# Product-key queries of three weight blocks as three products of rounded parts, keys behind the next block's half

## The reference, cut to what matters

```python
q = (xf @ wq).reshape(T, PEER_HEADS, 2, PEER_KEY_DIM)
s = jnp.einsum('thcd,ckd->thck', q, subkeys)
sv, si = lax.top_k(s, PEER_TOPK)
cand = (sv[:, :, 0, :, None] + sv[:, :, 1, None, :]).reshape(T, PEER_HEADS, 256)
cv, ci = lax.top_k(cand, PEER_TOPK)
...
act = jax.nn.gelu(jnp.einsum('cd,ced->ce', xc, u_tab[ec]))
return jnp.einsum('ce,ced->cd', act * gc, v_tab[ec])
```

## Time and profile before

| | us |
|---|---|
| median of three runs | 3874.69 (3873.38 to 3875.21) |
| span of the profiled execution | 3869.6 |
| TensorE busy (share of the span) | 3708.4 (96%) |
| VectorE busy | 1932.2 (50%) |
| ScalarE busy | 1122.8 (29%) |
| GpSimd busy | 311.1 (8%) |
| keys and queries of layer 0 | about 196 to 256 |
| same stage of layer 1 | about 1275 to 1334 |

### The profile page before, as it was taken

How to read it: one execution, slowest core, us unless ns; L and a number is a source line. 1 busy time by engine, 2 the same in 40 slices (tenths; PEclk the granted TensorE clock), 3 DMA queues, 4 the chain that set the end, 5 groups by cost and what they waited for, 6 DMA issues and landing times.

```text
span 3869.6 us, 59400 instructions
## 1 busy us (share of the span) xinstructions
PE 3708.4 (96%) x25424; PEld 2645.2 (68%) x25424; DVE 1932.2 (50%) x3543; ACT 1122.8 (29%) x1721; POOL 311.1 (8%) x205
## 2 busy tenths in 40 slices
PE   8999999999999999999999999999899999999997
PEld 7789988898887799889888875666743333332333
DVE  5485667768655865676777424455612111111111
ACT  3223244444433232444444412333210000000011
POOL 0013200000000132000000000112100000000000
PEclk9899999999999999999999999999999999999999
DMA  5535344445545354344455331112379999999996
GB/s 197 216 136 169 131 148 160 175 160 179 174 175 186 142 167 139 135 172 168 160 184 178 135 116 74 68 66 87 113 317 427 427 427 428 428 427 427 428 428 277
DMA packets 81039, 846.48 MB, mean 219 GB/s; under 512 B 8896, under 2 KB 11072, under 8 KB 12512
## 3 DMA queue, kind: packets, MB, share of 16 engines
q1 hardware_dynamic: 80768, 842.60, 55.8%
HBM read 841.52 MB, written 1.05 MB: 218 GB/s over the span
## 4 chain that ended last, share of the span: by engine, by line
PE 80%; DMA 10%; DVE 7%; ACT 2%; issue 1%; POOL 0%; DVEq 0%; ACTq 0%; SPq 0%
PE bank L86 78%; DMA ring<-in_w_gu_dram 10%; DVE arena L122 2%; ACT arena L112 1%; PE bank L99 1%; DVE arena L190 1%; DVE arena L136 1%; DVE arena L184 1%; DVE arena L166 0%; DVE arena L154 0%; DVE arena L196 0%; DVE ring_rounded L122 0%; DVE arena L128 0%; DVE arena L130 0%; DMA ring<-in_w_inA_dram 0%
## 5 line engine op out<-in xcount | busy, mean ns | idle before, releaser
L86 PE MATMUL bank<-arena 128*128 128x32 bf16 (+9 forms) x10068 | 970.5, 297 | 44.1 <-DVE arena L122 17.2
L86 PEld LDWEIGHTS bank<-arena 128*128 128x128 bf16 (+4 forms) x10068 | 550.7, 124 | 458.7 <-issue 335.1
L122 DVE TENSOR_TENSOR arena<-arena 128x512 bf16<-128x512 bf16 (+5 forms) x898 | 559.2, 657 | 53.2 <-ACT arena L112 37.6
L112 ACT ACTIVATE arena<-bank 128x256 f32<-128x256 f32 (+2 forms) x443 | 202.7, 457 | 1272.9 <-PE bank L86 1043.5
L86 PE MATMUL bank<-ring,arena 128*64 128x512 f32 (+1 forms) x1968 | 503.7, 596 | 39.9 <-DMA ring<-in_w_gu_dram 36.2
L86 PE MATMUL bank<-xT,ring 128*128 128x256 f32 (+1 forms) x2208 | 458.1, 365 | 14.3 <-DMA ring<-in_w_inA_dram 11.3
L86 PE MATMUL bank<-xhi,uhi 128*128 128x256 f32 x1552 | 454.3, 293 | 14.5 <-DVE arena L128 8.7
L86 PE MATMUL bank<-xlo,uhi 128*128 128x256 f32 x1552 | 438.2, 282 | 0.0
L86 PE MATMUL bank<-xhi,ring_rounded 128*128 128x256 f32 x1552 | 436.0, 281 | 0.0
L86 PEld LDWEIGHTS bank<-xT,ring 128*128 128x128 f32 x2208 | 388.7, 193 | 60.9 <-issue 11.6
L86 PEld LDWEIGHTS bank<-ring,arena 128*64 128x64 f32 (+1 forms) x1968 | 170.6, 145 | 362.0 <-issue 282.6
(11 more groups left out here) (137 smaller groups left out, 2949.3 us busy)
## 6 DMA issues: line engine op xcount, KB each, us to landing
ring<-in_w_gu_dram SPq DMA_DIRECT2D x97, 2048.0 KB, 23.8
ring<-in_peer_u_dram SPq DMA_DIRECT2D x128, 1024.0 KB, 6.7
ring<-in_peer_v_dram SPq DMA_DIRECT2D x128, 1024.0 KB, 5.1
arena<-in_w_dn_dram SPq DMA_DIRECT2D x62, 2048.0 KB, 22.3
arena<-in_w_gu_dram SPq DMA_DIRECT2D x43, 2048.0 KB, 22.4
ring<-in_w_hg_dram SPq DMA_DIRECT2D x14, 2048.0 KB, 8.2
ring<-in_w_mod_dram SPq DMA_DIRECT2D x12, 2048.0 KB, 8.2
ring<-in_w_inA_dram SPq DMA_DIRECT2D x8, 2048.0 KB, 8.0
```

The lines of the kernel that those rows point to most:

```text
L86: i = self.e.matmul(o, l, r, start=start, stop=stop)
L112: self.e.activation(o, i, f, scale=scale, **kw).then_inc(self.sem, 1)
L122: self.e.tensor_tensor(o, a, b, op).then_inc(self.sem, 1)
```

## The change

The weight blocks 1 to 3 of the queries are multiplied as parts, as the parted expert blocks are: ScalarE copies each half, rounded, to a new place in the arena (`q_hi`, laid over the expert layer's activations, which aren't in use yet), and a subtraction writes the rest over the weights in the ring. VectorE does it for block 1, ahead of its choosing; GpSimd for blocks 2 and 3. TensorE does the keys of a block behind the first half of the next block, and the keys of block 3 behind expert block 0. ScalarE's queue is reordered to fit, and expert blocks 0 and 2 are rounded before block 3's second half of queries.

```diff
+        def pe_query_parts(l, j, hf):
+            b, (s, n) = route_banks.take("q", l, j, hf)
+            P.wait_ge(s, n)
+            P.wait_ge(*at["x split", l])
+            P.wait_ge(*at["wq split", l, j, hf])
+            hi, lo = q_hi[j - 1][:, :, hf * 256:hf * 256 + 256], query_low(l, j, hf)
+            for k in range(2):
+                cs = slice(k * 128, k * 128 + 128)
+                P.mm(b[:, k * 256:k * 256 + 256], [(w[:, dc, cs], x[:, dc, :]) for dc in range(8)
+                                                   for w, x in ((hi, xhi), (hi, xlo), (lo, xhi))])
...
         def pe_peer(l):
             after_stage(P, "mix", l)
-            for j in range(4):
-                for hf in range(2):
-                    pe_query(l, j, None if j else 1, hf)
-                for tk in range(2):
...
+            for hf in range(2):
+                pe_query(l, 0, 1, hf)
+            for j in range(1, 4):
+                pe_query_parts(l, j, 0)
+                pe_keys(l, j - 1)
+                pe_query_parts(l, j, 1)
+            pe_stage1(l, 0)
+            pe_keys(l, 3)
             P.mark("routed", l)
-            P.wait_ge(*at["x split", l])
-            for c in range(TURNED):
+            for c in range(1, TURNED):
                 pe_stage1(l, c)
...
+        def split_query(q, l, j, hf):
+            q.wait_ge(*at["wq high", l, j, hf])
+            q.tt(query_low(l, j, hf), query_of(l, j, hf), q_hi[j - 1][:, :, hf * 256:hf * 256 + 256].bitcast(F32), SUB,
+                 lag=FREE)
+            q.mark("wq split", l, j, hf)
...
             V.mark("x split", l)
+            for hf in range(2):
+                split_query(V, l, 1, hf)
             for j in range(4):
                 dve_choose(l, j)
...
+        def act_split_query(l, j, hf):
+            A.wait_ge(*at["landed", ("wq", l, j)])
+            A.act(q_hi[j - 1][:, :, hf * 256:hf * 256 + 256], query_of(l, j, hf), ACT.Copy)
+            A.mark("wq high", l, j, hf)
...
             A.mark("x high", l)
-            for j in range(4):
...
-            act_split_u(l, 0)
-            act_split_u(l, 2)
+            act_split_query(l, 1, 0)
+            act_query(l, 0, 0)
+            act_split_query(l, 1, 1)
+            act_query(l, 0, 1)
+            for hf in range(2):
+                act_split_query(l, 2, hf)
+            for j in range(1, 4):
+                act_query(l, j, 0)
+                act_key_scores(l, j - 1)
+                if j == 1:
+                    for hf in range(2):
+                        act_split_query(l, 3, hf)
+                if j == 3:
+                    act_split_u(l, 0)
+                    act_split_u(l, 2)
+                act_query(l, j, 1)
+            act_key_scores(l, 3)
...
             G.mark("keys listed", l)
+            for j in (2, 3):
+                for hf in range(2):
+                    split_query(G, l, j, hf)
             for c in parted:
```

More of the change, by code:

```diff
@@ L315, in build @@
         with nc.sbuf_tensor("arena", [128, ARENA], F32) as arena:
+            pass
+        with nc.sbuf_tensor("arena_rounded", [128, ARENA], F32R) as arena_r:
             pass
@@ L1131, in build @@
         g3 = ea[:, :, 2, :].rearrange("p t (h k) -> p t h k", h=8)
+        q_hi = [arena_r[:, H0 + i * PIECE:H0 + (i + 1) * PIECE].rearrange("p (c n) -> p c n", c=8) for i in range(3)]
+        assert H0 + 3 * PIECE <= ARENA - SPLIT + 4608 - 12736
         acc = bank[0:4]
@@ L1238, in pe_stage2, with query_of, query_low, pe_keys @@
                     ring.back(P, "vt", l, c // 2)
+        def query_of(l, j, hf):
+            return ring.of("wq", l, j)[:, 0:PIECE].rearrange("p (c n) -> p c n", c=8)[:, :, hf * 256:hf * 256 + 256]
+        def query_low(l, j, hf):
+            i = ring.place.get(("wq", l, j), 0) * HALF
+            return ringr_t[:, i:i + PIECE].rearrange("p (c n) -> p c n", c=8)[:, :, hf * 256:hf * 256 + 256]
+        def pe_query_parts(l, j, hf):
[8 more added lines that the diff above has]
+                                                   for w, x in ((hi, xhi), (hi, xlo), (lo, xhi))])
+            P.mark("q", l, j, hf)
+            if hf:
+                ring.back(P, "wq", l, j)
+        def pe_keys(l, j):
+            for tk in range(2):
+                b, (s, n) = route_banks.take("key", l, j, tk)
+                P.wait_ge(s, n)
+                P.wait_ge(*at["query", l, j])
+                for k in range(4):
+                    P.mm(b[:, k * 128:k * 128 + 128], [(pq[j % 2][:, k, tk * 128:tk * 128 + 128], sk[:, k % 2, :])])
+                P.mark("key", l, j, tk)
         def pe_query(l, j, tk, hf):
@@ L1242, in pe_query @@
             w = ring.of("wq", l, j)[:, 0:PIECE].rearrange("p (c n) -> p c n", c=8)
-            t0, t1 = (0, 256) if tk is None else (tk * 128, tk * 128 + 128)
+            t0, t1 = tk * 128, tk * 128 + 128
             if tk != 1:
@@ L1486, in act_split_u, with act_query, act_key_scores @@
             A.mark("u high", l, c)
+        def act_split_query(l, j, hf):
+            A.wait_ge(*at["landed", ("wq", l, j)])
+            A.act(q_hi[j - 1][:, :, hf * 256:hf * 256 + 256], query_of(l, j, hf), ACT.Copy)
+            A.mark("wq high", l, j, hf)
+        def act_query(l, j, hf):
+            A.wait_ge(*at["q", l, j, hf])
+            if j >= 2:
+                A.wait_ge(*at["key", l, j - 2, 1])
+            A.act(pq[j % 2][:, 2 * hf:2 * hf + 2, :],
+                  route_banks.of("q", l, j, hf)[:, :].rearrange("p (k t) -> p k t", k=2), ACT.Copy)
+            route_banks.back(A, "q", l, j, hf)
+            if hf:
+                A.mark("query", l, j)
+        def act_key_scores(l, j):
+            for tk in range(2):
+                A.wait_ge(*at["key", l, j, tk])
+                A.act(ps_[j][:, tk, :, :], route_banks.of("key", l, j, tk)[:, :].rearrange("p (k t) -> p k t", k=4),
+                      ACT.Copy)
+                route_banks.back(A, "key", l, j, tk)
+            A.mark("key scores", l, j)
         def act_split_p(l, c):
```

## The result

The changed kernel takes 3884.07 us (median of 16 runs, 3876.77 to 3889.56). The kernel before has a median of 3876.18 in its 16 runs beside them, and of 3875.21 without the one that took 4731.22 us, which is left out of the ratio as a slow run. The ratio is 1.0023, 95% interval 1.0015 to 1.0030: 0.23% slower.

A forecast was written before the change was run, and what follows sets the result against it. TensorE is 96% busy, but VectorE's choosing meets it at the turn with 2.7 us to spare in layer 0. Later turns 4.1 + 3.6 plus clock 4.0 make 11.7 us longer: 3869.6 + 11.7 + 5.1 = 3886.4, range 3868 to 3897.

The forecast's parts named there:

- TensorE's walk: Routing stage, layer 0: TensorE's rows with parts and new order, reaching the turn at 320.6, 16.7 us earlier.
- a block as parts: Query products on TensorE: 96 part products take 11.3 us instead of 13.8, 2.5 us less per block.
- the order: TensorE's reordered keys and expert block 0: waits of 0.69 and 4.36 us and the slow clock (1.4) go.
- The later keys: Block 0's keys behind a half block: VectorE starts choosing at 211.9, 4.95 us later than 206.96.
- The first pass's holds: VectorE's first choosing pass: GpSimd's long splits hold its cast and tensor operation, 3.4 + 4.6 = 8.0 us.
- Later holds: VectorE's later choosing passes in layer 0: GpSimd's expert splits hold it 0.9, 2.3, 0.6 and 2.4, together 6.2 us.
- The clock: TensorE's slow restart behind a 21 us wait at each turn: 2.0 us, ends 0 and 3; 4.0 for both layers.
- (C): Rival: TensorE's gain holds in full, 2 x 16.7 us less, 3841.3; needs the choosing off the path; chance 0.04.
- (A): Rival: VectorE gets the port between GpSimd's third and fourth split, hold 3.4 instead of 8.0; 3877.2; chance 0.22.
- (B): Rival: GpSimd's long splits don't hold VectorE's first pass, later holds as few as layer 1's; 3864.6; chance 0.09.
- (E): Rival: a late rounding makes TensorE wait between parts; time is the forecast's; chance within the forecast case's 0.53.
- (D): Rival: worse phases, later holds of 9.4 and clock cost of 3 per layer; 3894.8; chance 0.12.

The follow-up runs named there:

- turn28: Changed kernel with the turn of the chosen gates behind 28 expert blocks, not 24; ratio 0.9972 to the kernel before.
- turn32: Changed kernel with the turn of the chosen gates behind 32 expert blocks, not 24; 3841.7 us, ratio 0.9920 to the kernel before.
- pool_pieces: Changed kernel with each of GpSimd's four splits of 2048 columns made in two of 1024; ratio 1.0023 to the kernel before.
- keys_at_once: Changed kernel with keys of blocks 0 to 2 ahead of the next block's first half, scores copied at once; ratio 1.0041 to the kernel before.
- parts_block1: Changed kernel with query blocks 2 and 3 as f32 products again, without GpSimd's long splits, key order kept; ratio 1.0003 to the kernel before.
- block1_at_once: parts_block1 with the keys ahead of the next block's first half; ratio 0.9993 to the kernel before.
- no_holds: parts_block1 with expert blocks 0 to 23 all as f32 products too, against GpSimd work during the choosing; ratio 0.9982 to the kernel before.
- no_holds_at_once: no_holds with the keys ahead of the next block's first half; 3878.34 us in a single run.

## Why the prediction was right, step by step

The forecast was 3886.4 us by a sum of +11.7; measured is 0.23% of 3876, +8.9 us (5.8 to 11.6).

TensorE's walk held to a tenth: keys 0 at 13.1 behind the rounding (13.0), expert block 0 at 47.1 (47.2), the turn reached 16.7 earlier (16.7). Its parts were less exact and made up for each other: a block as parts is worth 2.3 us and not 2.5 (its 96 products take 11.6 us, not 11.3), the order 9.9 and not 8.6 (four waits cost 0.95 us each, not 0.7). In layer 1 TensorE gained 17.2, where I had taken layer 0's 16.7. That the two misses cancel is luck.

The later keys: 4.95 forecast, 4.8 measured. The first pass's holds: 8.0 forecast, 7.5 measured; the splits take 4.57 us each and not 4.7. The value I chose between 0 and 9 was the one at which the nearest row was taken literally: held until the instruction under way ends, twice. That a hold lasts for the whole instruction is also what the Trainium skill, SBUF — State Buffer, section "SBUF: two separate sides", says of the shared ports, and the runs here now show it for splits of 2.3 and of 4.57 us. Later holds: 6.2 forecast, 5.8 measured, but as a sum only: I had four (0.9, 2.3, 0.6, 2.4) and there are five (1.1, 0.3, 2.2, 0.6, 1.7), so that this term came so near is partly luck. The gates' way to the turn, 1.7 us, was right too, the exponential's table being loaded ahead of its wait. So the turns came 3.0 and 2.5 us later where 4.1 and 3.6 stood in the sum. The clock: 2.0 per layer taken, 1.4 and 1.5 measured, with the restart slow from its first instruction. By these rows the sum is 3.0 + 2.5 + 2.9 = 8.4, beside 8.9 measured. The restart isn't a constant: by the same distance it costs 1.3 to 2.5 us in the other kernels that wait at the turn (2.5 in layer 0 of turn28, behind only 8.7 us).

Of the rivals, (C), the full gain, was the one that an engine's busy share would suggest: 96% of the span. It failed for the reason given, 2.7 us of slack in one layer; and turn32 shows that the place of the turn decides it. (A) and (B) needed shorter holds, and there were none; and pool_pieces, which made (A)'s short hold real, stayed at 1.0023 where (A)'s time is a ratio of 1.0006, so (A)'s time would have been missed even with its condition met. (E) did not occur: from 190 us to the turn the trace has no wait of TensorE but the one of 19.7. (D)'s worse phases did come, in keys_at_once. What I had not seen is how far the parts of my own sum depended on each other: the holds of the first pass and the later ones are not two terms that add, and the later ones hang on TensorE's own walk through the time of the expert splits. In pool_pieces the 3.5 us taken from the one came back whole in the other, in parts_block1 2.6 of 7.5, in block1_at_once 3.0 of 4.8.

## What to carry to other kernels

Where two chains meet at a point in a hand-written order, read the slack of the one that isn't changed before crediting the one that is; if it is small, move the meeting point together with the change. Here that was one number, and it turned 0.23% slower into 0.80% faster than the kernel before. And before giving GpSimd a batch of work, look at what VectorE does beside it. In every trace here a cast, a copy within SBUF, a scalar operation or a tensor operation with two inputs in SBUF that came while a split ran waited for its end (0.20 us became up to 3.37, 0.69 up to 5.02); searches and reductions kept their short durations.

## What the runs showed of the hardware that was not expected

VectorE's choosing falls into step with GpSimd's splits. An operation that comes during a split goes on when the split ends, whenever it came, so an earlier arrival at the same split is worth nothing behind it (57.96 and 57.95 above). With a split every 6.29 us the gates came at 144.2 us from the rounding of x in two kernels whose first passes differed by 3.5 us. Without long splits a start 4.8 us earlier was worth 1.7 (137.6 for 139.3); with them, and with all expert splits 2.9 us later, it was worth -2.9. Without GpSimd the same 4.8 us were worth 4.8 to the logits (115.1 - 1.5 and 113.5 us of length). It goes the other way too: in the kernel before, the same choosing takes 125.3 us in layer 0 and 120.0 in layer 1, where the later expert splits stand only 0.5 us later.

A wait of 0.69 us between TensorE's products costs 0.95 us of its walk: three of them make 2.86 us between the turns of no_holds and no_holds_at_once (136.43 and 139.29), one makes 0.95 from keys to keys.

And the same program takes up to 8 us more or less to the first rounding of x (187.9 to 196.1 us in the thirteen profiles) through the stretches in which TensorE's clock falls: in the two mixings shown the same work met 0.50 at different places. Against effects of 0.2% one profile of each kernel says nothing by its span; its distances within the stage can be read, for they repeat to 0.1 us in the two layers of every kernel that waits at the turn.
